# Forgetting attention in a two-block model: where the next pair's queries and keys leave PSUM, and where projection slices stand against the waits

## The reference

```python
def fox_mixer(h, w_in, b_f, q_gain, k_gain, w_out):
    proj = h @ w_in
    q, k, v, g, f_logit = jnp.split(proj, [1024, 2048, 3072, 4096], axis=-1)
    log_f = jax.nn.log_sigmoid(f_logit + b_f)
    qh = rms_norm(to_heads(q, 16), q_gain)
    kh = rms_norm(to_heads(k, 16), k_gain)
    vh = to_heads(v, 16)
    o = fox_attention(qh, kh, vh, log_f.transpose(0, 2, 1))
    # logit[t,s] = q_t.k_s / sqrt(64) + c[t] - c[s], c = cumsum(log f), s <= t; softmax; times v
    o = o.transpose(0, 2, 1, 3).reshape(b, s, 1024)
    return (o * jax.nn.silu(g)) @ w_out
```

## Time and profile before

| | |
|---|---|
| median of 3 runs | 2381.26 us (2379.41 to 2382.15) |
| the profiled execution | 2380.49 us, span 2378.4 us |
| TensorE busy | 2213.0 us (93%) |
| VectorE, ScalarE, GpSimd busy | 1187.6, 851.2, 548.9 us |
| mean granted clock of TensorE | 0.970 |
| longest chain, share of TensorE | 81% |

### The profile page before, as it was taken

One profiled execution on the slowest core, in us unless ns is written; L12 is line 12 of the kernel. 1 busy time (PEld: TensorE's weight loads), 2 busy tenths in 40 slices (PEclk: granted clock), 3 DMA queues, 4 the chain that ended last, 5 costly groups with the idle time before them and its releaser, 6 DMA issues.

```text
span 2378.4 us, 29133 instructions
## 1 busy us (share of the span) xinstructions
PE 2213.0 (93%) x11168; PEld 1860.4 (78%) x11168; DVE 1187.6 (50%) x1486; ACT 851.2 (36%) x1265; POOL 548.9 (23%) x292
## 2 busy tenths in 40 slices
PE   4899999999998799999899979999999999988996
PEld 4778889888887599899688867877877877867885
DVE  6963331634333533434435454566566566575444
ACT  3136653112022322432313133554544545553311
POOL 1322222333432121222143222111111111112320
PEclk9999999999998799999899989999999999999998
DMA  8112222113330210110221121111011011013101
GB/s 335 48 49 67 71 71 80 47 43 106 133 124 27 89 45 27 45 36 29 112 82 38 42 98 55 36 44 44 24 54 45 18 53 53 18 44 133 45 18 71
DMA packets 36660, 154.59 MB, mean 65 GB/s; under 512 B 4161, under 2 KB 4161, under 8 KB 35810
## 3 DMA queue, kind: packets, MB, share of 16 engines
q1 hardware_dynamic: 23840, 93.52, 11.3%
q10 hardware_dynamic: 12738, 59.87, 7.1%
HBM read 128.15 MB, written 21.04 MB: 63 GB/s over the span
## 4 chain that ended last, share of the span: by engine, by line
PE 81%; DVE 12%; issue 4%; ACT 2%; DMA 0%; DVEq 0%; SPq 0%; ACTq 0%
PE psG L311 21%; PE psG L312 20%; PE psG L313 20%; PE psA L311 3%; PE psA L312 2%; PE psA L313 2%; PE psA L1804 1%; PE psA L1803 1%; PE psA L1778 1%; PE psA L1704 1%; DVE FDR L2095 1%; DVE M L871 1%; PE psA L399 1%; DVE AL L849 1%; DVE AL L824 1%
## 5 line engine op out<-in xcount | busy, mean ns | idle before, releaser
L311 PE MATMUL psG<-AH,WH 128*128 128x512 f32 x2112 | 857.5, 406 | 56.7 <-DVE AL L824 18.4
L312 PE MATMUL psG<-AL,WH 128*128 128x512 f32 x2112 | 833.7, 395 | 0.0
L313 PE MATMUL psG<-AH,WL 128*128 128x512 f32 x2112 | 833.0, 394 | 0.0
L298 POOL TENSOR_SCALAR WH<-RAW 128x1024 fp32r<-128x1024 f32 x144 | 159.4, 1107 | 1743.0 <-PE psG L311 1299.6
L311 PEld LDWEIGHTS psG<-AH,WH 128*128 128x128 f32 x2112 | 402.9, 191 | 145.4 <-issue 33.2
L313 PEld LDWEIGHTS psG<-AH,WL 128*128 128x128 f32 x2112 | 402.2, 190 | 88.5
L312 PEld LDWEIGHTS psG<-AL,WH 128*128 128x128 f32 x2112 | 403.4, 191 | 70.8
L300 POOL TENSOR_TENSOR WL<-RAW,WH 128x1024 fp32r<-128x1024 f32 x144 | 389.6, 2705 | 12.0
L2085 DVE TENSOR_TENSOR FTL<-PF,FTH 128x512 fp32r<-128x512 f32 x192 | 109.8, 572 | 156.5 <-ACT FTH L1966 155.2
L1959 ACT ACTIVATE PF<-psA,PB 128x512 f32<-128x512 f32 x192 | 111.2, 579 | 118.2 <-PE psA L1806 64.5
L2095 DVE RECIPROCAL FDR<-psA 64x128 f32<-64x128 f32 x128 | 118.2, 940 | 31.7 <-PE psA L313 30.0
(11 more groups left out here) (318 smaller groups left out, 2945.3 us busy)
## 6 DMA issues: line engine op xcount, KB each, us to landing
RAW<-w_tiles SPq DMA_DIRECT2D x144, 512.0 KB, 3.4
gates<-SIG ACTq DMA_DIRECT2D x16, 512.0 KB, 2.9
park<-X ACTq DMA_DIRECT2D x2, 4096.0 KB, 11.1
CB<-fox_c ACTq DMA_DIRECT2D x16, 512.0 KB, 4.4
X<-xT SPq DMA_DIRECT2D x4, 1024.0 KB, 12.3
WADA_SCALE<-w_ada SPq DMA_DIRECT2D x1, 4096.0 KB, 24.3
WADA_SHIFT<-w_ada SPq DMA_DIRECT2D x1, 4096.0 KB, 34.2
WADA_GATE<-w_ada ACTq DMA_DIRECT2D x1, 4096.0 KB, 16.4
```

The costliest lines, as they stand in the source:

```text
L298: nc.gpsimd.tensor_scalar(WH[:, i, :], RAW[:, i % RAW_SLOTS, :], 1.0, 0.0, ALU.mult, ALU.add).then_inc(w_high, 1)
L311: first = nc.tensor.matmul(out, wh, xh, start=start, stop=False)
L312: nc.tensor.matmul(out, wh, xl, start=False, stop=False)
L313: return first, nc.tensor.matmul(out, wl, xh, start=False, stop=stop)
```

## The change

Four things, all in the forgetting attention's looped pairs.

The lists: FILL_MAX holds 20 slices where it held 17, FILL_SUM 28 where it held 31. In FILL_SUM pieces 0, 1, 3, 6 and 8 have one slice less, pieces 4 and 23 one more. In head 0 of the maximum phase a score's slices now stand ahead of its waits, with one for each score from 1 to 7; score 8 has one slice, where it had none.

ScalarE takes queries and keys out of PSUM in four parts each, two of squares and two of copy, 512 columns wide: the queries behind pieces 1, 2, 3 and 5, the keys behind 12, 13, 14 and 15.

VectorE normalises the next queries ahead of the last division's fourth reciprocal.

```diff
-    FILL_MAX = [0, 0, 1, 1, 0, 1, 1, 1, 2, 0, 0, 2, 1, 1, 1, 1, 1, 1, 2]
-    FILL_SUM = [3, 2, 1, 2, 1, 1, 2, 2, 2, 1, 1, 1, 1, 1, 1, 1, 1, 1, 1, 1, 1, 1, 1, 1]
+    FILL_MAX = [0, 1, 1, 1, 1, 1, 1, 1, 2, 0, 1, 2, 1, 1, 1, 1, 1, 1, 2]
+    FILL_SUM = [2, 1, 1, 1, 2, 1, 1, 2, 1, 1, 1, 1, 1, 1, 1, 1, 1, 1, 1, 1, 1, 1, 1, 2]
...
-    Q_AT, K_AT = filled(16), filled(32)
+    Q_AT, K_AT = [1, 2, 3, 5], [12, 13, 14, 15]
+    assert Q_AT[0] > filled(16) and K_AT[0] > filled(32)
...
         for i in range(NB):
+            fill(fill_max[i])
             if i == 0:
                 pe.wait_ge(fqk_ready, p * 2 + 1)
                 pe.wait_ge(fdup_ready, p * 2 + 1)
...
             else:
                 pe.wait_ge(fmax_ready, p * N_S + (i - 1))
-            fill(fill_max[i])
             score(i, 0, (i + 1) % 2)
...
+    def act_fox_raw_part(act, p, x, n):
+
+        if n == 0:
+            act.wait_ge(psum_full, p * 4 + (U_FOX + x + 1))
+        to, f = (FSQ[x][:, :], ACT.Square) if n < 2 else (FN[x], ACT.Copy)
+        hs = slice((n % 2) * HALF, (n % 2 + 1) * HALF)
+        l = nc.scalar.activation(to[:, hs], fox_buf(x)[:, hs], f)
+        if n == 1:
+            l.then_inc(fsq_ready, 1)
+        elif n == 3:
+            l.then_inc(psum_free, 1)
...
             exp(j)
             high(j)
-            if more and j == Q_AT:
-                act_fox_raw(act, nxt, 0)
-            if more and j == K_AT:
-                act_fox_raw(act, nxt, 1)
+            for x, at in enumerate((Q_AT, K_AT)):
+                if more and j in at:
+                    act_fox_raw_part(act, nxt, x, at.index(j))
...
         divide(1, 1, 2)
         if more:
             dve_fox_rex(dve, 1)
+            dve_fox_norm(dve, nxt, 0)
         divide(1, 1, 3)
-        if more:
-            dve_fox_norm(dve, nxt, 0)
         divide(1, 1, 4)
```

## The result

| | before | changed |
|---|---|---|
| median | 2380.34 us (2378.98 to 2382.15, 4 runs) | 2344.9 us (2344.35 to 2345.68, 4 runs) |
| span of the profiled execution | 2378.4 us | 2343.0 us |
| mean granted clock of TensorE | 0.970 | 0.971 |

The ratio is 0.9849, 95% interval 0.9837 to 0.9861: 35.4 us faster, against a forecast of 35.6. The added code moves the lines: in the changed kernel a score is line 1780 and its mask 1782 (1778 and 1780 before), and the lines of VectorE lie 13 further down, those of ScalarE 14.

The account below looks back on a forecast made before the run. TensorE was taken as the bound, losing time in a few waits; terms of -4.11 us a pair, 28.8 over seven, plus 6.8 for the clock made 35.6 us off 2380.49: 2345 us forecast, range 2338 to 2350 (chance 0.57).

Parts of the forecast that it names:

- Keys, -2.19: At piece 9, quartering and moving the keys' copies removes TensorE's whole wait for FTL: 2.19 us saved a pair.
- piece 11, +0.67: At piece 11, GpSimd's subtraction for the values' tile holds VectorE's low half: 0.67 us lost a pair.
- Head 0, -1.87: Maximum phase, head 0: slices ahead of waits bring row 0 0.49 us earlier with two more slices: 1.87 us saved a pair.
- between the heads, -0.69: One slice ahead of score 8 hides under TensorE's waits before scores 8 and 9: 0.69 us saved a pair.
- Spread, -0.72: At the pair's end, normalising queries earlier removes the wait ahead of the keys' spreading: 0.72 us saved a pair.
- Piece 0, +0.69: Behind row 1, TensorE waits at piece 0 for the time of one missing slice: 0.69 us lost a pair.
- The clock, -6.8: Half-clocked stretches behind the piece 9 wait, in four of seven pairs, go with it: 6.8 us saved in all.
- rival 1: The half clock stays after a remaining wait at piece 0 or 11: 2352 us, chance 0.12.
- Rivals 2 to 5: Low half of 10 caught, 2356 us (0.13); quarters not hiding, 2379 (0.07); clock falling long, 2408 (0.03); no effect, 2380 (0.04).
- Rivals 4 and 5: Clock falls long in the maximum phase, up to 2408 us, chance 0.03; waits only move, 2380 us, chance 0.04.

Follow-up runs that it names:

- e8: The kernel before with only the quarter-wise copies of queries and keys and their places added: 2363.4 us, ratio 0.9925 to before.
- e5: The changed kernel with the values' tile counted as begun by its 14th slice, not its first: 2340.2 us, ratio 0.9827 to before.
- e2: The changed kernel with the keys taken out whole, behind piece 12: 2346.2 us, ratio 0.9848 to before.
- e12: The changed kernel with the values' tile counted as begun late (e5) and the keys taken out whole behind piece 9: 2346.5 us, ratio 0.9859 to before.
- e3: The changed kernel with head 0's slices behind their waits again, same numbers of slices: 2347.9 us, ratio 0.9857 to before.
- e4: The changed kernel with the queries' normalisation behind the fourth reciprocal again: 2347.2 us, ratio 0.9855 to before.
- e6: The changed kernel with three slices at piece 0 and one at piece 23: 2339.1 us, ratio 0.9826 to before.
- e1: The changed kernel with the keys taken out whole, behind piece 8 as before: 2381.3 us, ratio 1.0002 to before.
- e9: The changed kernel with the keys' quarters behind pieces 9 to 12 in place of 12 to 15: 2344.4 us, ratio 0.9854 to before.

## Why the prediction was right

*The sum.* Forecast were 4.11 us a pair; 89.81 to 85.48 is 4.33. Times seven that is 30.3, and the four half-clocked stretches give 91.4 - 89.8 = 1.6 us each, 6.5: 36.8 in the seven pairs. 37.0 were measured there. The whole time shows 35.4, since 1.6 us were lost outside: the first silu comes 0.9 us later, the stretch behind the last takes 0.7 more. So the terms are right to some tenths of a microsecond each, but that the whole comes within 0.2 us is luck: the pairs gave 1.4 us more than forecast, and the rest of the program, put at nothing, took 1.6 back.

*Keys, -2.19, and piece 11, +0.67.* Shown by e8 (1.74 us a pair with nothing but the quarters, where 1.5 was expected) and by e5 (0.74 back when GpSimd is moved). 0.2 us of e8's gain were not in my sum; the wait at piece 1, 0.18 us from start to start in the kernel before, is one that I had left out. But my reason was half the cause. I named ScalarE's 2 us; e2 and e12 show that they alone cost 0.4 to 1.2 us, by their place. The old place also held ScalarE 1.5 us for the tile's last matmul; that number stands in brackets in the earlier trace rows, and I didn't use it. And the low half of piece 9, for which TensorE waited, was itself held by GpSimd's subtraction, 1.23 us for 0.69; I used that row for the new collision and not for the old wait. For the forecast it made no difference: the new places are free of the wait for the tile and of the late exponential, and GpSimd's hold, which moves to piece 11, has its own term.

*Head 0, -1.87, and between the heads, -0.69.* Row 0 came at 9.59. Not tried apart: e3 turns only the order back, 0.41 us. What is left of 4.33 without e8's 1.74 and e4's 0.69 is 1.9 us for the lists and their order, piece 0 included; by my terms it is 1.87 + 0.69 - 0.69. This is a remainder, and no run shows how it divides between the two terms. The cover ahead of score 9 was mis-sized: I took 0.1 us to be left, 0.39 was. I had counted idle times (0.33 + 0.50); from start to start the two waits were some 1.2 us, and less a slice that is the 0.5 now measured. The gain is the slice in either case, since the cover held.

*Spread, -0.72.* e4: 0.69. ScalarE's cover was 0.2 us by the layout and measures 0.17 from the copy's end to score 0.

*Piece 0, +0.69.* The wait is 0.8 us from start to start, as laid out; e6 takes it down to the 0.12 us that the kernel before had there.

*The clock, -6.8.* No stretch at 1.2 GHz is left in the looped pairs (rival 1 fell); e1 brings them back with the wait. The 6.8 us are four stretches, the number in the one profiled execution that I had; how many there are in others was not looked at.

*Rivals 2 to 5.* The low half of 10 got in ahead of the subtraction with 0.13 us to spare (0.14 forecast). The quarters take 0.58 us and hide, in wide pieces too (e9). Rivals 4 and 5 didn't happen.

## What to carry to other kernels

Where a program repeats itself to a hundredth, laying out one period by hand, with durations and latencies from neighbouring rows, gives not only the gain but the next two waits; count a wait from start to start of the waiting engine, since idle time behind modelled ends hides 0.15 us and more of each. Before cutting a long instruction in pieces, look at what the instruction waits for: where it waits, everything behind it on its engine waits too, and here a better place for the whole instruction (e2) gave all but 0.4 us of what place and cut gave together. And ask what a moved matmul starts elsewhere: here it was a weight split on GpSimd that held VectorE and so cost TensorE 0.7 us a pair, and the cure was one count made later.

## What the runs showed of the hardware

The low half FTL of 512 columns, a VectorE instruction with two SBUF inputs, ended 0.55 us behind GpSimd's subtraction when it began while that ran, whatever was left of it: 1.23 us long for 0.68 of overlap, 1.66 in the changed kernel, 2.33 in e1, the same in all seven pairs of each. One that began in the last hundredths of the rounding got in before the subtraction, which was then late itself (2.82 us for 2.37). An instruction with one of its inputs in PSUM was not held: the addition `X<-X,psG` that began at 2146.93 us in the changed kernel, 1.98 us into a subtraction that ran on for 1.13 us behind its end, took 1.21 us, as it did elsewhere (1.22).

The clock fell to 1.2 GHz behind an idle time of 2.04 us in four of seven pairs and behind 3.83 us in seven of seven (e1); behind 0.91 us or less it never fell in the looped pairs of any run here. That the idle time is the cause is argued from these three, as nothing else in those pairs differed in kind. The length of one wait isn't all of it: in the last pair of the changed kernel, whose head 0 has no slices, the clock fell at 2064.91 us behind waits of 0.34, 0.42 and 0.48 us that stood close together among scores (granted clock 1.00 from 2060.0 to 2064.9 us, 0.50 from 2065 to 2070), and ahead of the longer wait that follows.
